# Raw memory rows, an earlier pair of weights and later sums in a two-layer decoder kernel

## What is computed

```python
def _memory_heads(q_flat, mem, ln_g, w_kv, g_qn, g_kn):
    q = _rms(q_flat.reshape(b, s, N_MEM_HEADS, MEM_HEAD_DIM), g_qn)
    kv = (_rms(mem, ln_g) @ w_kv).reshape(b, mem.shape[1], N_MEM_HEADS, 2 * MEM_HEAD_DIM)
    k = _rms(kv[..., :MEM_HEAD_DIM], g_kn)
    v = kv[..., MEM_HEAD_DIM:]
    sc = jnp.einsum('bqhd,bkhd->bhqk', q, k).astype(jnp.float32) * (MEM_HEAD_DIM ** -0.5)
    p = jax.nn.softmax(sc, axis=-1)
...
            q, k, v = ...                     # 12 heads of 64 out of h @ sb_w_in
            o = _stick_breaking(q, k, v)      # layer 0
...
            q = _rms(q, mla_g_qn[j])          # layer 1: each head's 96 columns by their own mean square
```

## Time and profile before

| what | us |
|---|---|
| median of three runs | 2671.93 (2670.9 to 2675.89) |
| the profiled execution: time | 2675.89 |
| its span, first to last instruction | 2674.2 |
| PE busy | 2532.8 (95%) |
| DVE busy | 1729.3 (65%) |
| ACT busy | 1312.1 (49%) |
| POOL busy | 1119.3 (42%) |

### The profile page before, as it was taken

One profiled execution on the slowest core, in us unless ns is written; L12 is line 12 of the kernel. 1 busy time (PEld: TensorE's weight loads), 2 busy tenths in 40 slices (PEclk: granted clock), 3 DMA queues, 4 the chain that ended last, 5 costly groups with the idle time before them and its releaser, 6 DMA issues. The chain is left out here.

```text
span 2674.2 us, 37095 instructions
## 1 busy us (share of the span) xinstructions
PE 2532.8 (95%) x12000; PEld 2051.9 (77%) x12000; DVE 1729.3 (65%) x2659; ACT 1312.1 (49%) x2487; POOL 1119.3 (42%) x845
## 2 busy tenths in 40 slices
PE   6899999989999999999888989999799999999999
PEld 5777777667788888888676877777687888888887
DVE  5567778855865655478654277777748665665595
ACT  6467777744433333444554356666535333333443
POOL 2134445311465566555310432223003765665554
PEclk9899999999999999999989999999899999999999
DMA  3211110143222232674211100000152322323843
GB/s 127 55 32 32 32 33 9 32 173 111 79 98 102 96 112 87 228 236 147 83 38 37 34 16 22 23 21 21 49 183 98 115 98 91 109 102 131 291 129 118
DMA packets 182859, 242.74 MB, mean 91 GB/s; under 512 B 31440, under 2 KB 105936, under 8 KB 182736
## 3 DMA queue, kind: packets, MB, share of 16 engines
q1 hardware_dynamic: 182736, 241.19, 27.3%
HBM read 175.60 MB, written 65.54 MB: 90 GB/s over the span
## 5 line engine op out<-in xcount | busy, mean ns | idle before, releaser
L2255 POOL TENSOR_TENSOR l0s_run_lo<-l0s_run,l0s_run_hi 128x512 fp32r<-128x512 f32 (+2 forms) x120 | 143.5, 1196 | 216.4 <-DVE l0s_run_hi L2408 216.4
L471 POOL TENSOR_TENSOR l1f_wd_lo<-l1f_d,l1f_wd_hi 128x512 fp32r<-128x512 f32 x77 | 108.2, 1406 | 106.1 <-ACT l1f_wd_hi L546 106.0
L471 POOL TENSOR_TENSOR l0f_wd_lo<-l0f_d,l0f_wd_hi 128x512 fp32r<-128x512 f32 x77 | 110.5, 1439 | 97.4 <-ACT l0f_wd_hi L546 97.3
L84 PE MATMUL banks<-l1f_T_hi,l1f_op_hi 128*128 128x512 f32 x352 | 137.4, 390 | 0.9 <-DVE l1f_T_lo L691 0.9
L84 PE MATMUL banks<-l0f_T_hi,l0f_op_hi 128*128 128x512 f32 x352 | 137.4, 390 | 0.9 <-DVE l0f_T_lo L691 0.9
L86 PE MATMUL banks<-l0f_T_hi,l0f_op_lo 128*128 128x512 f32 x352 | 137.8, 392 | 0.0
L86 PE MATMUL banks<-l1f_T_hi,l1f_op_lo 128*128 128x512 f32 x352 | 137.8, 391 | 0.0
L85 PE MATMUL banks<-l1f_T_lo,l1f_op_hi 128*128 128x512 f32 x352 | 137.4, 390 | 0.0
L85 PE MATMUL banks<-l0f_T_lo,l0f_op_hi 128*128 128x512 f32 x352 | 137.4, 390 | 0.0
L433 POOL TENSOR_TENSOR l1f_s<-l1f_raw 128x512 f32<-128x512 f32 x44 | 66.4, 1510 | 153.5 <-DMA l1f_raw<-in_w_ffn_gu_dram 130.7
L503 ACT ACTIVATE l1f_op_hi<-l1f_s 128x512 fp32r<-128x512 f32 x88 | 55.2, 631 | 142.8 <-PE banks L86 141.0
(11 more groups left out here) (532 smaller groups left out, 8406.9 us busy)
## 6 DMA issues: line engine op xcount, KB each, us to landing
l0f_raw<-in_w_ffn_gu_dram SPq DMA_DIRECT2D x22, 1024.0 KB, 5.2
l1f_raw<-in_w_ffn_gu_dram SPq DMA_DIRECT2D x22, 1024.0 KB, 5.1
l0f_a_raw<-hidden_rows SPq DMA_DIRECT2D x77, 256.0 KB, 4.0
l1f_a_raw<-hidden_rows SPq DMA_DIRECT2D x77, 256.0 KB, 3.4
hidden_rows<-l0f_hid SPq DMA_DIRECT2D x44, 256.0 KB, 2.0
l0f_d<-in_w_ffn_down_dram SPq DMA_DIRECT2D x44, 256.0 KB, 5.1
hidden_rows<-l1f_hid SPq DMA_DIRECT2D x44, 256.0 KB, 2.0
l1f_d<-in_w_ffn_down_dram SPq DMA_DIRECT2D x44, 256.0 KB, 4.8
```

What stands on the lines that cost most here:

```text
L84: pe.matmul(out, l_hi, r_hi, start=first, stop=False, skip_group_check=True)
L471: pool.tensor_tensor(wd_lo[g % RING][:], held[HELD_AT[DOWN[p][1]]][i][:], as_f32(wd_hi[g % RING][:]), ALU.subtract).then_inc(wd_lo_done, 1)
L2255: pool.tensor_tensor(run_lo[x % NR][:, f:HALF], run[x % NR][:, f:HALF], as_f32(run_hi[x % NR][:, f:HALF]), ALU.subtract).then_inc(run_spli ...
```

## The change

- **First stage of layer 0.** PE transposes the memory rows as they were loaded; the row's factor is applied when DVE takes keys and values out of their banks. The memory's gain column and the weights are loaded ahead of x, the query weights ahead of the second half of x. Two of the four lower halves of the weights are made by DVE. ACT begins with the memory's upper halves and the weights; the squares come behind. PE makes keys and values ahead of turning x, both query units of the first half behind that, then turns the second half two chunks ahead of unit 2, and turns the keys ahead of unit 3. Layer 1's order stays.
- **First pair's weights.** `FirstWeights` loads, splits and lowers the query and key weights at the end of the first stage; `Ahead` keeps the value weights. The tiles' places change.
- **First pair's products** have new places in the jobs.
- **Latent heads.** "rq 0" goes from step 8 to 9, "kturn 0" from 9 to 10, "rq 1" and "qnorm 1" from 19 to 20.

```diff
             if not early:
                 for t in range(NM):
                     sp.dma_start(mem_x[:, t, :], mem_dram[t * P:(t + 1) * P, :]).then_inc(m_in[t], 16)
+                with nc.allow_non_contiguous_dma("gain"):
+                    sp.dma_start(m.mcol[:], gain_columns(ln_mem)).then_inc(mcol_in, 16)
+                for n in range(4):
+                    sp.dma_start(m.raw[n][:], kv_rows[:, 2 * n:2 * n + 2, :]).then_inc(w_in[n], 16)
                 for t in range(4):
                     sp.dma_start(x[:, t, :], x_dram[t * P:(t + 1) * P, :]).then_inc(x_in[t], 16)
-                for n in range(4):
...
+            sp.dma_start(m.wq_raw[:], q_rows).then_inc(wq_in, 16)
+            if not early:
+                with nc.allow_non_contiguous_dma("gain"):
                     sp.dma_start(m.gcol[:], gain_columns(ln)).then_inc(col_in, 16)
-            sp.dma_start(m.wq_raw[:], q_rows).then_inc(wq_in, 16)
...
+            if first:
+                first.load(sp, normed[1])
...
         def _(pool):
             if not early:
                 constants.on_pool(pool)
-                for n in range(4):
+                for n in (0, 2):
                     pool.wait_ge(w_hi_done, n + 1)
-                    pool.tensor_tensor(m.wkv_lo[n][:], m.raw[n][:], as_f32(m.wkv_hi[n][:]), ALU.subtract).then_inc(w_lo_done, 1)
+                    pool.tensor_tensor(m.wkv_lo[n][:], m.raw[n][:], as_f32(m.wkv_hi[n][:]), ALU.subtract).then_inc(wkv_lo_done[n], 1)
             pool.wait_ge(wq_hi_done, 1)
             pool.tensor_tensor(m.wq_lo[:], m.wq_raw[:], as_f32(m.wq_hi[:]), ALU.subtract).then_inc(wq_lo_done, 1)
+            if first:
+                first.lower(pool)
...
                     elif g and not early:
-                        act.wait_ge(squared[0], 4)
+                        act.wait_ge(m_squared, NM)
...
+            else:
+                act.wait_ge(mcol_in, 16)
+                upper_memory()
                 for n in range(4):
                     act.wait_ge(w_in[n], 16)
                     act.activation(m.wkv_hi[n][:], m.raw[n][:], ACT.Copy).then_inc(w_hi_done, 1)
...
+                act.wait_ge(constants.copied, 1)
+                squares(0)
+                for n in range(4):
+                    act.wait_ge(wkv_lo_done[n], 1)
+                upper_query_weights()
+                squares_of_memory()
+                act.wait_ge(col_in, 16)
+                upper_normed(0)
+                squares(1)
+                act.wait_ge(g_in, 48)
+                queries(0)
+                deviations_of_keys()
+                upper_normed(1)
+                upper_keys_and_values()
+                queries(1)
             stack((0, 2))
+            if first:
+                first.upper(act, 0)
             queries(2)
             deviations_of_queries(0)
+            if first:
+                first.upper(act, 1)
             queries(3)
             deviations_of_queries(1)
...
+            def sums_of_keys():
+                dve.wait_ge(kv_made, 1)
+                for t in range(NM):
+                    src = psum[4 + t][:].rearrange("p (h a d) -> p h a d", h=MEM_HEADS, a=2)
+                    dst = k32[:, t * MEM_HEADS:(t + 1) * MEM_HEADS, :, :]
+                    if early:
+                        last = dve.tensor_copy(dst, src)
+                    else:
+                        last = dve.tensor_scalar(dst, src, m.mrstd[:, t:t + 1], None, ALU.mult)
+                last.then_inc(k_chain, 1)
...
+            else:
+                for n in (1, 3):
+                    dve.wait_ge(w_hi_done, n + 1)
+                    dve.tensor_tensor(m.wkv_lo[n][:], m.raw[n][:], as_f32(m.wkv_hi[n][:]), ALU.subtract).then_inc(wkv_lo_done[n], 1)
+                normalise(0)
                 dve.wait_ge(m_root, 1)
                 dve.reciprocal(m.mrstd[:], m.mstd[:]).then_inc(m_inverse, 1)
                 dve.wait_ge(m_inverse, 1)
-                for t in range(NM):
-                    dve.tensor_scalar(mem_x[:, t, :], mem_x[:, t, :], m.mrstd[:, t:t + 1], None, ALU.mult).then_inc(m_normed, 1)
-                normalise(0)
-                dve.wait_ge(col_in, 32)
...
+                dve.wait_ge(col_in, 16)
+                lower_normed(0)
+                sums_of_keys()
+                normalise(1)
+                queries(0)
+                normalise_keys()
+                lower_normed(1)
+                lower_keys_and_values()
+                queries(1)
             stack((1, 3))
             queries(2)
             scales_of_queries(0)
...
             if not early:
                 pe.wait_ge(constants.made, 1)
-                pe.wait_ge(m_normed, NM)
+                for i in range(NM):
+                    pe.wait_ge(m_in[i], 16)
...
-            for c in range(ND):
-                turn(0, c)
-            for c in range(ND):
...
-            last.then_inc(kv_made, 1)
-            for c in range(ND):
-                project(0, c)
-            for c in range(ND):
-                turn(1, c)
-                project(1, c)
-            sums_of_queries(0)
-            pe.wait_ge(k_lo, 2)
-            for n in range(4):
-                turn_heads(n)
-            sums_of_queries(1)
-            for c in range(ND):
-                project(2, c)
...
+            else:
+                keys_and_values()
+                for c in range(ND):
+                    turn(0, c)
+                for c in range(ND):
+                    project(0, c)
+                for c in range(ND):
+                    project(1, c)
+                sums_of_queries(0)
+                for c in range(ND + 2):
+                    if c < ND:
+                        turn(1, c)
+                    if c >= 2:
+                        project(2, c - 2)
+                sums_of_queries(1)
+                turn_keys()
             for c in range(ND):
                 project(3, c)
             sums_of_queries(2)
...
-        self.w_hi = [place(f"w_hi{i}", 104 + 4 * i, [P, ND, P], F32R) for i in range(3)]
+        self.first_raw = [place(f"first_raw{i}", 128 + 4 * i, [P, ND, P]) for i in range(2)]
+        self.w_hi = [place(f"w_hi{i}", at, [P, ND, P], F32R) for i, at in enumerate((108, 112, 104))]
...
+class FirstWeights:
+
+
+
+    def __init__(self, tiles, sources):
+        self.t, self.sources = tiles, sources
+
+    def enter(self, sem):
+        self.loaded = [sem(f"first_loaded{i}") for i in range(2)]
+        self.hi_done, self.lo_done = sem("first_hi_done"), sem("first_lo_done")
+
+    def load(self, sp, normed):
+
+        sp.wait_ge(normed, 4)
+        for i in range(2):
+            sp.dma_start(self.t.first_raw[i][:], self.sources[i]).then_inc(self.loaded[i], 16)
+
+    def upper(self, act, i):
+        act.wait_ge(self.loaded[i], 16)
+        act.activation(self.t.w_hi[i][:], self.t.first_raw[i][:], ACT.Copy).then_inc(self.hi_done, 1)
+
+    def lower(self, pool):
+        for i in range(2):
+            pool.wait_ge(self.hi_done, i + 1)
+            pool.tensor_tensor(self.t.w_lo[i][:], self.t.first_raw[i][:], as_f32(self.t.w_hi[i][:]), ALU.subtract).then_inc(self.lo_done, 1)
...
-        self.pe_at = {3 + i: (i // 2, i % 2) for i in range(12)}
-        self.dve_at = {4: [0], 6: [1], 7: ["h0"], 8: [2], 9: ["h1"], 10: [3], 11: ["h2"], 12: [4], 13: ["h3"], 14: [5]}
+        self.pe_at = {0: (0, 1), 1: (2,), 3: (3,), 5: (4,), 6: (5,), 7: (6,), 9: (7,), 11: (8,), 12: (9,), 13: (10,), 15: (11,)}
+        self.dve_at = {0: [0], 4: [1], 5: ["h0"], 6: [2], 8: ["h1"], 9: ["h2"], 10: [3], 11: ["h3"], 12: [4], 15: [5]}
...
         if job == 2:
             for i in range(3):
-                sp.wait_ge(self.ahead.lo_done, i + 1)
+                if i == 2:
+                    sp.wait_ge(self.ahead.lo_done, 1)
                 sp.dma_start(self.t.raw[i][:], self.sources[i]).then_inc(self.next_in[i], 16)
...
     def pe(self, pe, at):
-        if at in self.pe_at:
-            n, part = self.pe_at[at]
+        for n, part in (divmod(m, 2) for m in self.pe_at.get(at, ())):
             what, half = self.UNITS[n]
             if part == 0 and n:
                 pe.wait_ge(self.emptied, n)
             i, cols = "qkv".index(what), slice(half * HALF, (half + 1) * HALF)
-            pe.wait_ge(self.ahead.lo_done, i + 1)
+            if i == 2:
+                pe.wait_ge(self.ahead.lo_done, 1)
...
-              6: ["kv 3", "knorm 0", "wk"], 7: ["q 1 0", "ksum 1", "q 1 1", "q 1 2", "knorm 1"], 8: ["ss 0", "rq 0"],
-              9: ["kturn 0"], 11: ["kturn 1"], 12: ["qnorm 0", "q 2 0", "wq 0"], 13: ["q 2 1", "v0"], 15: ["q 2 2"],
-              16: ["q 3 0"], 17: ["q 3 1", "q 3 2"], 18: ["wq 1", "kturn 2"], 19: ["ss 1", "rq 1", "qnorm 1"],
-              21: ["kturn 3"]}
+              6: ["kv 3", "knorm 0", "wk"], 7: ["q 1 0", "ksum 1", "q 1 1", "q 1 2", "knorm 1"], 8: ["ss 0"],
+              9: ["rq 0"], 10: ["kturn 0"], 11: ["kturn 1"], 12: ["qnorm 0", "q 2 0", "wq 0"], 13: ["q 2 1", "v0"], 15: ["q 2 2"],
```

(91 more changed lines are left out.)

101 lines of the change are left out of this document (47 added, 54 removed).

## The result

The changed kernel takes 2652.73 us (median of 4, 2651.05 to 2656.0), the kernel before beside it 2673.91 (median of 4): ratio 0.9917, 95% interval 0.9903 to 0.9931. So it is faster by some 21 to 22 us (0.8%); 2647 was forecast. The profiled execution took 2651.14 with a span of 2649.4.

What follows compares the result with a forecast made beforehand. TensorE (PE) was taken to set the span. First stage -9.6, memory attention -8.0 and latent heads -7.8 sum to -25.4: 2650.5 against the profiled execution, 2646.5 against the median, stated as 2647; range 2637 to 2659.

Steps and rivals of the forecast that it cites:

- First stage, -9.6 forecast: Layer 0's stage before memory attention: products end at 28.1 instead of 40.65, stage at 69.5 instead of 79.1; bounds -3 and -13.
- The low clock ahead of them, +2 us: Key and value products: 2 us added to their 11.0 because PE pauses 4 us ahead of them.
- estimated 1.3: First stage: DVE's time for each lower half of weights 1 and 3, ending at 14.7 and 16.8.
- 41.4 were forecast: First stage after the products: 38.45 + 6.0 turning x - 4.6 wait and cold stretch + 1.5 turning keys.
- VectorE and POOL exclude each other: Rival, first stage: x's normalisation blocked by POOL's query weights, last two tiles end near 30, 2649; chance 0.1.
- Attention, -8.0 forecast: Layer 0's memory attention: the first pair's re-placed products gain 11.0 and give back 3; bounds -3 and -11.
- The 11.0 to be had: Memory attention: 7.0 of PE waits plus 5.5 lost to low clock, less 1.5 for scores that stay cold.
- the 3 given back: Memory attention: PE reaches units before DVE has emptied the one bank; 3 us, bounds 0 and 8.
- The rival of the copies: Rival, memory attention: copies set the pace, DVE's chain costs 8 us more, -3 there, 2652; chance 0.12.
- Latent heads, -7.8 forecast: Five of six pairs: ten PE waits of 0.78 for ACT's copy of the sums go; bounds 0 and -8.5.
- only moves: Rival, latent heads: the wait only moves to the turns of keys, gain 0 there, 2654; chance 0.08.
- my own sign of being wrong: Latent heads: forecast called wrong if a pair still takes 64 us; one of three such signs.

## Why the prediction was nearly right, step by step

- **First stage, -9.6 forecast, -7.7 measured.** The chain was right, its steps late: column landed at 7.0 (7.3 forecast), but ACT's first upper half began only at 7.87, behind a table load of 1.28 us that the sum left out, and ACT was free at 12.3 (11.3), products at 15.9 (15.1) and through at 29.5 (28.1). The low clock ahead of them, +2 us, is there: 12 products 0.2 us too long each are 2.4. Another size that failed is DVE's "estimated 1.3" for a lower half, and with it the times of both engines: DVE's own part was 1.1, but it stood behind POOL's each time and took 2.97 on the mean. That cost nothing itself, since PE was slower still. From the first turn of x to the stage's end 41.4 were forecast; from 29.96 to 71.4 (the attention's start less the 1.1 us between 79.1 and 80.2 before) it is 41.4; whether each term of that sum came out was not measured. So the 1.9 us are 0.8 at the start, 0.6 in the products and 0.5 of wait.
- **"VectorE and POOL exclude each other"** was right, and my reading against it, "by the rows it is slowed, 2.4 times, not stopped", was wrong: it took a mean for a rate. In the kernel before, the four scalings behind 1794 ns are two of 0.75 us, ahead of POOL's work, and two of 2.84 and 2.83, each ending 0.55 us after one of POOL's subtractions. In the changed kernel one stood for all that was left of POOL's 4.9 us. The last tile ended at 29.9, as the rival has it ("near 30"). It cost 0.5 us and not 2, because PE's products ended late as well, at 29.5. The Trainium skill's page SBUF — State Buffer (Who interferes with whom) says that the second one is blocked in full; the trace agrees.
- **Attention, -8.0 forecast, -8.0 measured.** The 11.0 to be had and the 3 given back are both in the windows. The waits that give back are other ones in part: 1.5 for a lower half of p, 1.2 for a query unit's copy and 0.2 for a key unit's, where 2 were forecast. The 1.4 at the last output was there before as well. The clock did what the forecast has it do: it was at its lower level for 19.1 us of the attention before and for 4.3 after. The rival of the copies did not come; PE's first 17.7 us hold 17.67.
- **Latent heads, -7.8 forecast, -3.7 measured.** This is the mis-sized term. The removal was right (10.4 to 1.8, even more than the forecast 2.6). Of the new one-step spacings I wrote "I take 0, since the step from 11 to 12 has the same spacing and no wait". Measured: 0.5 at the second keys' turn in each of five pairs (2.5), and 0.6 at scores behind the later rq 1, four times (2.2), where ACT has the sums' logarithm and exponential among those of the attention. How much work of PE stands between two steps I did not work out for the places where it mattered, and the one place that I looked at was no model for them. My rival "only moves" had the mechanism and one of the two places; it was true for about half of the gain. A pair took 63.9 us, so my own sign of being wrong, "if a pair of the latent heads still takes 64 us", was met in all but 0.1 us.
- **Sum.** Against the median the two misses, 1.9 and 4.1, are the 6 us between 2647 and 2653. That they fit so well is partly chance: the three parts are 19.4, the medians differ by 21.2, and the median of the kernel before rose by 2.0 against the one I counted from. That the profiled executions differ by 24.8, close to the forecast 25.4, is luck: 5.4 of it is in stages that the change does not touch. Run again, the changed kernel's profile had a span of 2653.0, with 229.2 and 51.9 in two of them.
- **Open.** The 14 profiles settle part of what the untouched stages do. The opening took 173.8 to 174.0 us in six of them, where the trace's clock records add up to 30.7 us at the lower level inside it; 175.4 and 175.7 in two, with 34.1; and 177.7 to 177.8 in six, with 36.9 or more. So its two lengths go with the clock. Stick-breaking goes with it too: 519.2 to 519.8 in five profiles with 12.9 to 13.7 us at the lower level, 520.9 to 521.0 in five with 19.2 or 19.3, and 522.4 to 522.9 in four with 20.7 to 21.4. It does not go with the dealing: one of the 519 has the old places (519.4), one of the 522 the new ones (522.4). In layer 0's down-projection 229.3 and 227.0 have the same 6.8 us, so there the cause stays open. And no run shows why the clock falls once more or less in stages whose code is the same.

## What to carry to other kernels

Price a moved step at its new neighbours: whoever shares its buffer one step behind inherits the wait, and a place elsewhere with the same spacing proves nothing unless as much work stands between. Where long elementwise jobs of DVE and POOL overlap, read each instruction's own duration and not the group's mean: here 1839 ns was three times 0.75 us and once 5.1. And keep the one whose result isn't urgent out of the other's way; 4.4 us of DVE came back by moving one POOL subtraction by 2.7 us. And for parts under 0.3% compare the stage in traces, not the medians: the latent part is 3.7 and 3.8 us in two pairs of traces, where the times gave 7.8 (by the ratios) and 2.6 (by the medians; 4.3 by the ratios).

## What the runs showed of the hardware that was not expected

- The granted clock prints 1.00 for the first 15.93 us and on to 21, while products start 0.43 us apart, nearly twice the 0.23 of later ones (columns as in the windows of the result's section):
```profile
15.93:21.10 5.17, 5.17 (x12) 4.10 (x13) 4.26 (x2) 4.88 (x10) 3.17 (x1) 1.00 1.12 331
```
  The trace has no clock record before 21.05 us, just where the pace changes. So here the duration of a product tells the level (1.2 GHz), the printed clock does not. The Trainium skill's page TensorE: Matmul & The Clock Gate (What's actually happening) has the low level as the default; the durations agree, the printed clock does not.
- DVE and POOL did not share: whichever of a DVE scaling or subtraction and a POOL subtraction came second stood until the first was done, for up to 4.4 us (5107 ns for a scaling that takes 750).
- A short fall of the clock comes and goes with changes made far ahead of it: in every other pair in one kernel (1.2 us each), and in the opening, 3.9 us from its short to its long form. In one profile it cancelled a real gain of 4 us.
- The 4 KB gain column landed 5.3 us after its issue with 1 MB ahead of it, and 11.0 with about 5 MB ahead.
